# A Fourier block in float32: its products split into three passes, and a residual update moved to GpSimd

## What is computed

```python
def fourier_mix(h, w_o):
    B_, L_, D_ = h.shape
    hg = h.astype(jnp.float32).reshape(B_, L_, FOURIER_GROUPS, FOURIER_GROUP_CH)
    f = jnp.fft.fft2(hg, axes=(1, 3), norm="ortho").real
    return f.reshape(B_, L_, D_).astype(h.dtype) @ w_o
...
def post_norm_update(x, y, mod, j, g, b):
    gate = mod[:, 3 * j + 2][:, None, :]
    return layer_norm(ALPHA * x + gate * y, g, b)
```

## Time and profile before

| what | value |
|---|---|
| median of 3 executions | 2187.61 us (2186.68 to 2189.37) |
| the profiled execution | 2184.68 us |
| its span | 2182.7 us |
| mean granted clock of PE in it | 0.993 |
| PE busy | 2103.3 us, 15744 matmul records |
| DVE busy | 1617.4 us |
| ACT busy | 972.5 us |
| POOL busy | 2.3 us, 8 instructions |

### The profile page before, as it was taken

One profiled execution on the slowest core, in us unless ns is written; L12 is line 12 of the kernel. 1 busy time (PEld: TensorE's weight loads), 2 busy tenths in 40 slices (PEclk: granted clock), 3 DMA queues, 4 the chain that ended last, 5 costly groups with the idle time before them and its releaser, 6 DMA issues. The chain is left out here.

```text
span 2182.7 us, 37144 instructions
## 1 busy us (share of the span) xinstructions
PE 2103.3 (96%) x15744; PEld 1874.4 (86%) x15744; DVE 1617.4 (74%) x2326; ACT 972.5 (45%) x1345; POOL 2.3 (0%) x8
## 2 busy tenths in 40 slices
PE   7999999999999999999999799989999999999998
PEld 5899999887899999977999689889799986768886
DVE  3887877777787788775887778676787776667556
ACT  3434534427543454344434466344454454215443
POOL 0000000000000000000000000000000000000000
PEclk9999999999999999999999999999999999999999
DMA  9866688430689768733988211300388822305541
GB/s 394 331 240 248 235 313 337 155 116 1 248 350 360 298 274 323 309 134 145 366 327 307 67 59 59 136 23 3 126 333 349 339 98 78 116 31 210 209 177 39
DMA packets 65812, 450.83 MB, mean 207 GB/s; under 512 B 7959, under 2 KB 9240, under 8 KB 12696
## 3 DMA queue, kind: packets, MB, share of 16 engines
q1 hardware_dynamic: 65688, 449.11, 53.4%
HBM read 448.03 MB, written 1.05 MB: 206 GB/s over the span
## 5 line engine op out<-in xcount | busy, mean ns | idle before, releaser
L541 PEld LDWEIGHTS banks<-ffn_h_split,ffn_weights_split 128*128 128x128 f32 x6336 | 769.6, 192 | 13.4 <-DVE ffn_weights_split L632 4.7
L541 PE MATMUL banks<-ffn_h_split,ffn_weights_split 128*128 128x256 f32 x6336 | 773.6, 284 | 7.3 <-DVE ffn_h_split L653 6.0
L826 DVE TENSOR_TENSOR ffn_weights_split<-weight_ring,ffn_weights_split 128x2048 fp32r<-128x2048 f32 x223 | 510.4, 2289 | 222.2 <-ACT ffn_weights_split L715 222.2
L715 ACT CAST ffn_weights_split<-weight_ring 128x2048 fp32r<-128x2048 f32 x223 | 424.0, 1901 | 162.7 <-PE banks L559 153.1
L559 PE MATMUL banks<-ffn_weights_split,ffn_hidden_split 128*128 128x512 f32 x1512 | 356.8, 392 | 2.4 <-DVE ffn_hidden_split L752 2.4
L559 PEld LDWEIGHTS banks<-ffn_weights_split,ffn_hidden_split 128*128 128x128 f32 x1512 | 280.9, 189 | 59.2 <-DVE ffn_hidden_split L752 2.8
L782 DVE CUSTOM_DVE_ANT_0 weight_ring<-weight_ring,first_arena,cols 128x1024 f32<-128x1024 f32 x196 | 240.5, 1280 | 0.4 <-ACT first_arena L725 0.4
L679 ACT ACTIVATE ffn_arena<-banks 128x256 f32<-128x256 f32 x132 | 50.6, 383 | 417.3 <-PE banks L541 417.3
L514 PE MATMUL banks<-ffn_h_split,ffn_weights_split 128*128 128x512 f32 x352 | 124.7, 399 | 0.2 <-DVE ffn_h_split L653 0.2
L516 PE MATMUL banks<-ffn_h_split,ffn_weights_split 128*128 128x256 f32 x352 | 98.7, 280 | 0.0
L121 ACT CAST weight_ring_split<-weight_ring 128x2048 fp32r<-128x2048 f32 x34 | 64.5, 1905 | 56.1 <-DMA weight_ring<-in_weights 38.4
(11 more groups left out here) (414 smaller groups left out, 2632.2 us busy)
## 6 DMA issues: line engine op xcount, KB each, us to landing
weight_ring<-in_weights SPq DMA_DIRECT2D x407, 1024.0 KB, 5.0
first_arena<-in_norm_rows SPq DMA_DIRECT2D x12, 512.0 KB, 7.2
first_arena<-in_c_rows SPq DMA_DIRECT2D x4, 512.0 KB, 11.9
first_arena<-in_ctx_rows SPq DMA_DIRECT2D x2, 1024.0 KB
h<-in_ctx SPq DMA_DIRECT2D x1, 1024.0 KB, 17.2
side<-in_x SPq DMA_DIRECT2D x1, 1024.0 KB
x<-in_x_rows SPq DMA_DIRECT2D x1, 1024.0 KB
hyena_tables<-in_hy_filt SPq DMA_DIRECT2D x1, 1024.0 KB
```

The lines of the kernel that those rows point to most:

```text
L541: last = nc.tensor.matmul(bank[:, half * T:half * T + T], w[:, x, sl], hs[:, k, y, :], start=(k == 0 and x + y == 0), stop=(k == DT - 1 an ...
L715: nc.scalar.copy(wsplit[:, c % S, 0, :], raw).then_inc(self.split_hi.sem, 1)
L826: nc.vector.tensor_tensor(wsplit[:, c % S, 1, :], core.wbuf[:, (self.first + at(c)) % NSLOT, :], wsplit[:, c % S, 0, :].bitcast(F32), ALU. ...
```

## The change

In the Fourier block every product but those of the first feature group is made in three passes from split operands. Three new tensors hold high and low parts: `fourier_table_split` (the table), `fourier_h_split` (groups 1 to 3 of `h`) and `fourier_uv_split` (`uv`). ACT makes each high part by a cast (that of `uv` in place of the copy), DVE each low part by a subtraction. `features_whole` is the first group, in plain float32. PE waits for low parts only, by their number in a fixed order (`FOURIER_LOW`). DVE's body no longer refreshes `x`: POOL has a body of its own that does, with the same two instructions (`refresh.on`). ACT's and DVE's other work of the block stands later in their orders.

```diff
     def dve(self, dve, r):
-
-        nc, row = self.core.nc, self.rows[:, r, :].unsqueeze(1).broadcast_to([P, TT, D])
+        self.on(dve, self.core.nc.vector, r)
+
+    def on(self, eng, engine, r):
+
+        row = self.rows[:, r, :].unsqueeze(1).broadcast_to([P, TT, D])
...
-        nc.vector.tensor_tensor(self.x[:, :, :], self.x[:, :, :], row, ALU.mult if r == 0 else ALU.add)\
+        engine.tensor_tensor(self.x[:, :, :], self.x[:, :, :], row, ALU.mult if r == 0 else ALU.add)\
             .then_inc(self.steps.sem, 1)
...
+FOURIER_LOW = {n: i + 1 for i, n in enumerate(("table", "h1", "uv00", "uv01", "h2", "h3", "uv10", "uv11", "uv20", "uv21", "uv30", "uv31"))}
...
+    PASSES = ((0, 0), (0, 1), (1, 0))
...
+        @block.gpsimd
+        def _(pool):
+            refresh.on(pool, nc.gpsimd, 0), refresh.on(pool, nc.gpsimd, 1)
+
         @block.tensor
         def _(pe):
+            def lows(name):
+                pe.wait_ge(low.sem, low.base + FOURIER_LOW[name])
+
+            def features_whole():
+                for t in range(TT):
+                    for k in range(2):
+                        last = nc.tensor.matmul(core.ps[t][:, :], h[:, k, t * P:t * P + P], both(cs[:, k, 0:2, :]),
+                                                start=(k == 0), stop=(k == 1))
+                    last.then_inc(uv_ready.sem, 1)
+
             def features(g):
+                if g == 1:
+                    lows("table")
+                lows(f"h{g}")
                 for t in range(TT):
                     if g >= 2:
-                        pe.wait_ge(uv_copied.sem, uv_copied.base + 2 * (g - 2) + t + 1)
+                        lows(f"uv{g - 2}{t}")
                     for k in range(2):
-                        last = nc.tensor.matmul(core.ps[2 * (g % 2) + t][:, :], h[:, 2 * g + k, t * P:t * P + P],
-                                                cs[:, k, 0:2, :].rearrange("p a n -> p (a n)"),
-                                                start=(k == 0), stop=(k == 1))
+                        for n, (x, y) in enumerate(PASSES):
+                            last = nc.tensor.matmul(core.ps[2 * (g % 2) + t][:, :], hs[:, 2 * g + k, x, t * P:t * P + P],
+                                                    both(css[:, y, k, 0:2, :]), start=(k + n == 0), stop=(k == 1 and n == 2))
                     last.then_inc(uv_ready.sem, 1)
...
         @block.scalar
         def _(act):
-            early.act_weight(act, 0)
+            def h_high(g):
+                nc.scalar.copy(hs[:, 2 * g:2 * g + 2, 0, :], h[:, 2 * g:2 * g + 2, :]).then_inc(high.sem, 1)
+
+            act.wait_ge(tables.sem, tables.base + 32)
+            nc.scalar.copy(css[:, 0, :, :, :], cs).then_inc(high.sem, 1)
+            h_high(1)
             for n in range(2 * G):
                 g, t = n // 2, n % 2
                 if n == 2:
+                    h_high(2), h_high(3)
+                    early.act_weight(act, 0)
+                if n == 4:
                     early.act_weight(act, 1)
...
         @block.vector
         def _(dve):
-            refresh.dve(dve, 0), refresh.dve(dve, 1)
-            early.dve_weight(dve, 0)
...
+            dve.wait_ge(high.sem, high.base + 1)
+            nc.vector.tensor_tensor(css[:, 1, :, :, :], cs, css[:, 0, :, :, :].bitcast(F32), ALU.subtract).then_inc(low.sem, 1)
+            h_low(1)
+            uv_low(0)
+            h_low(2), h_low(3)
+            uv_low(1)
+            early.dve_weight(dve, 0)
+            evacuate(0)
+            uv_low(2)
+            early.dve_weight(dve, 1)
+            evacuate(1)
+            uv_low(3)
+            context.dve_variance(dve)
+            evacuate(2), evacuate(3)
             context.dve_reciprocal(dve)
```

More of the change, by code:

```diff
@@ L1489, in attention, with fourier @@
     core.stage_done()
-def fourier(core, h, out, cs, uv, refresh, context, early, tables):
+FOURIER_LOW = {n: i + 1 for i, n in enumerate(("table", "h1", "uv00", "uv01", "h2", "h3", "uv10", "uv11", "uv20", "uv21", "uv30", "uv31"))}
+def fourier(core, h, out, cs, split, refresh, context, early, tables):
     nc = core.nc
@@ L1499, in fourier @@
     f_ready, f_copied = core.counter("fourier_out_ready"), core.counter("fourier_out_copied")
+    high, low = core.take("operand_high", 4), core.take("operand_low", len(FOURIER_LOW))
+    css, hs, uv = split["table"], split["h"], split["uv"]
     G = D // 256
     pair = lambda g: core.ps[4 + g % 2][:, :].rearrange("p (m t) -> p m t", m=2)
+    both = lambda x: x.rearrange("p a n -> p (a n)")
+    PASSES = ((0, 0), (0, 1), (1, 0))
     with core.block() as block:
@@ L1526, in tokens @@
                         for t in range(TT):
[L1527 to L1530, removed]
+                            for x, y in PASSES:
+                                last = nc.tensor.matmul(core.ps[4 + g % 2][:, m * T:m * T + T],
+                                                        uv[:, g % 2, t, x, part * T + m * P:part * T + m * P + P],
+                                                        css[:, y, t, 2 * part, :], start=(n == 0), stop=(n == 11))
+                                n += 1
                 last.then_inc(f_ready.sem, 1)
             pe.wait_ge(tables.sem, tables.base + 32)
-            features(0)
+            features_whole()
             for g in range(G):
@@ L1559, in _, with h_low, uv_low, evacuate @@
         def _(dve):
-            refresh.dve(dve, 0), refresh.dve(dve, 1)
-            early.dve_weight(dve, 0)
[L1562 to L1567, removed]
+            def h_low(g):
+                dve.wait_ge(high.sem, high.base + g + 1)
+                at = slice(2 * g, 2 * g + 2)
+                nc.vector.tensor_tensor(hs[:, at, 1, :], h[:, at, :], hs[:, at, 0, :].bitcast(F32), ALU.subtract)\
+                    .then_inc(low.sem, 1)
+            def uv_low(g):
+                for t in range(TT):
+                    dve.wait_ge(uv_copied.sem, uv_copied.base + 2 * g + t + 1)
+                    nc.vector.tensor_tensor(uv[:, g % 2, t, 1, :], core.ps[2 * (g % 2) + t][:, :],
+                                            uv[:, g % 2, t, 0, :].bitcast(F32), ALU.subtract).then_inc(low.sem, 1)
+            def evacuate(g):
                 dve.wait_ge(f_ready.sem, f_ready.base + g + 1)
@@ L3253, in first_block @@
                 run(core, project, ffn_a, ffn_b)
-            with phase("fourier", 2048, False):
-                uv = carve(2, TT, 2, T)
+            with nc.sbuf_tensor("fourier_table_split", [P, 2, 2, 3, T], F32R) as table_split, \
+                    nc.sbuf_tensor("fourier_h_split", [P, DT, 2, T], F32R) as fourier_hs, \
+                    nc.sbuf_tensor("fourier_uv_split", [P, 2, TT, 2, 2 * T], F32R) as uv_split:
+                split = dict(table=table_split, h=fourier_hs, uv=uv_split)
                 context = ContextNorm(core, xn, o, vec(2, 1, 1), vec(2, 0, 1), (scale_1, norm("norm1", 2)[0]), tail_small)
                 early = Early(core, side_lo[:, :, :].rearrange("p (k y) t -> p k y t", y=2), 2, False, [(0, 0), (1, 0)])
-                fourier(core, hf, hf, cs, uv, Refresh(core, x, rows), context, early, tables)
+                fourier(core, hf, hf, cs, split, Refresh(core, x, rows), context, early, tables)
                 core.stage_done()
```

15 lines of the change are left out of this document (6 added, 9 removed).

## The result

The changed kernel took 2194.1 us in the median of 16 executions (2190.63 to 2198.75), the kernel before 2188.63 beside it (16 executions, 2185.23 to 2190.54). The ratio is 1.0027, with a 95% interval of 1.002 to 1.0033: slower by some 5.5 us (4.4 to 7.2 by the interval), where 4.2 less were forecast. 2194.1 lies outside the range of 2181.8 to 2190.0 us. Its profiled execution took 2192.56 us at a mean granted clock of 0.988.

What follows compares the result with a forecast made beforehand. The prediction took PE's chain of matmul groups to bound the Fourier block. 4.4 us less PE work minus 0.2 of semaphore delays, the residual costing nothing, gave 4.2 us less: 2187.6 to 2183.4 us, range 2181.8 to 2190.0.

Steps and rivals of the forecast that it cites:

- PE's work: Fourier block's products: split feature groups take 2.74 us, token groups 2.88, together 4.4 us less PE time.
- What has to be ready: Fourier block: ACT's highs and DVE's lows come before PE wants them; costed at 0.2 us of semaphore delays.
- The residual: Refresh of x on POOL: two passes of 4.2 us end well before the block does; costed at nothing.
- rival 2: POOL first at the block's start holds the table's and h 1's lows: 3.3 us slower, 2190.9 us; chance 0.12.
- A rule against the change: Skill's rule that DVE instructions with two SBUF inputs and SBUF-reading GpSimd ones block each other; would give rival 1 or 2.
- the two rivals with turns: Rival 1 and rival 2, in both of which POOL and DVE take turns by whole instructions in the Fourier block.
- Rival 1: POOL, delayed by its ISA instruction, holds DVE's lows in mid-block: gain all but gone, 2187.3 us; chance 0.25.
- Rival 3: No slow start of PE's clock at the Fourier block's border: a gain of 5.6 us, 2182.0 us; chance 0.10.
- Rival 4: POOL ends last, over 20 us ahead of its first addition; 10 us beyond give 2193.4 us; chance 0.05.

Runs made afterwards that it cites:

- e4: The changed kernel with x refreshed on DVE in two free places, the second ring weight's low moved later, POOL without work; 2185.23 us, ratio 0.9982 to the kernel before.
- e3: The changed kernel, with POOL's refresh waiting until DVE has made its last low with two SBUF inputs; 2185.02 us, ratio 0.9984 to the kernel before.
- e6: e4 plus four POOL memsets of 128x2048 from the block's start into a scratch tensor that nobody reads; 2184.88 us in the profiled execution.
- e7: e6 with POOL's four memsets replaced by four copies of the table (128x1536, one SBUF input) into scratch; 2188.52 us in the profiled execution.
- e8: The changed kernel, with DVE making the lows of uv 0 (one PSUM operand) ahead of the table's and h 1's; 2194.38 us in the profiled execution.
- e2: The kernel before with only the refresh of x moved to POOL, products still plain float32; 2188.81 us, ratio 1.0 to the kernel before.
- e5: The changed kernel with POOL's refresh in four additions of 128x1024 instead of two of 128x2048; 2186.78 us, ratio 1.0001 to the kernel before.
- e1: The changed kernel with x refreshed first on DVE, as before, and nothing on POOL in the block; 2187.65 us, ratio 0.9992 to the kernel before.

## Why the prediction was wrong

**PE's work: right.** Features 2.75 us a group (988.59 to 991.34) where 2.74 stood, tokens 2.87 (991.34 to 994.21) where 2.88 stood, and 4.37 us less for the block without POOL (e4).

**What has to be ready: right without POOL.** In e3, at full clock, PE waited 0.31 us where 0.6 stood for a clock of 1.00 from the start, and DVE's lows were 1.76 and 0.68 us. The part called 1.2 us to spare "thin", but only against the clock.

**The residual: this step failed.** It said "Costed at nothing", and looked at one thing alone, whether POOL would be done before the block's end. It was, by 28 us. What it left out is what POOL does to DVE meanwhile: h 1's low ended 11.1 us behind the block's start, where PE wanted it after 3.67, and that cost 7.3 us of idle time and 2.4 us of slow clock (e3 against the change). The rivals had this hold. One of the two reasons given against rival 2 was the ISA instruction ahead of POOL's first addition that "may hold POOL back". Its two records took 11 ns each, and POOL began 0.06 us behind PE. The duration taken for a pass, 4.2 us, was near: 4.53.

**A rule against the change: weighed too lightly.** The other reason was that no row shows any blocking: the trace of before has none in which POOL reads while DVE reads two SBUF operands. But a row that doesn't exist speaks for neither side, and rival 2 was given 0.12. If the engines take turns and POOL is not late, the prediction's own pass of 4.2 us puts the end of h 1 low at 979.7 us, past the 976.4 that decides. So nearly all hung on whether the engines take turns, and the larger chance of the two rivals with turns (0.25) went to a delay of POOL for which no row stood either. The range then ended at 2190.0 us, below the rival's own 2190.9. The Trainium skill ("SBUF — State Buffer", section "Who interferes with whom") says that such a DVE instruction contends with a GpSimd instruction that reads SBUF, and not with one that only writes. The runs agree on each part: memsets beside lows of 1.76 us (e6), copies beside lows of 2.98 (e7), a low with one operand in PSUM at 0.69 (e8).

**Rival 2, term by term.** It had h 1 low end 979.7 - 968.8 = 10.9 us behind the block's start; it ended after 11.1. It had 5.7 us of idle; there were 7.6, because this block had no slow start at its border, so PE arrived at 3.67 and not at 5.2 us. It added a slow start of 1.76 behind the idle; the stretch there cost 2.4. From the full-clock block of e2: 33.28 - 4.4 + 7.6 + 2.4 = 38.9, measured 39.08, so 5.8 us more. The rival's sum of 3.3 was against a block with a slow start; against the profiled one the block grew by 4.13. The medians are 5.5 apart and the ratio gives 5.9; how many executions of before have the slow start isn't known, so the medians can't check the sum more closely than that.

**Rivals 1, 3 and 4.** Rival 1 had the same turns, only later in the block; POOL wasn't late. The hold that it describes did occur in e5, where the lows of h 2 and h 3 took 4.5 us together, and PE didn't wait for them. Rival 3's missing slow start did occur in the profiled execution, but was eaten by the idle time. Rival 4: POOL ended at 979.85, 28.5 us ahead of the last early products' end.

Two versions beat both kernels: e3 (0.9984) and e4 (0.9982). They can't be told from each other. Their gain, 3.5 to 3.9 us by these ratios, is what the forecast promised for a change that has POOL at the block's head.

What stays open: what decides whether PE's clock is low after the idle of 1.9 us at the block's border (it was in the profiled executions of before, e4, e5 and e7, not in those of after, e1, e2, e3, e6 and e8); and how the executions that weren't traced divide between the two starts, which would decide why e1, whose block is 1.8 us longer than e2's at the same start, shows no loss in its median (the intervals of the two ratios overlap).

## What to carry to other kernels

Before work that reads SBUF is moved to GpSimd, list the DVE instructions that run in the same stretch and read two SBUF tensors, and find the one that PE wants first. Each can be held by a whole GpSimd instruction, in turns; the cost is the hold less the time to spare, and it is nothing where that is large (e2) and was several us in the change, where the forecast had 1.2 to spare and a full clock left none. Place the GpSimd work behind the urgent ones with one wait (e3), or keep it on DVE at a place with time to spare (e4); and where PE would idle as long as in e1 (3.4 us) or in the change (7.6), add the slow clock behind the idle, some 2.4 us in this block.

## What the runs showed of the hardware that I had not expected

- A small size is no protection. In e3 two 128x1 instructions on DVE (L1163, all operands in SBUF) took 3.42 us together during POOL's second pass; in e4, with POOL idle, they took 0.35:

```profile
992.61 0.35 DVE L1163 SCALAR_TENSOR_TENSOR small<-small 128x1 f32<-128x1 f32 x2
```

- The turns alternated wherever both engines had an instruction waiting: in the change DVE's low went between POOL's two passes and POOL's second pass went between two lows. In e8, where no low with two SBUF operands had been issued when the first pass ended, POOL's two passes ran back to back, 9.11 us, and the change's took 10.51.
- Idle times of 3.36 (e1), 7.59 (the change) and 7.86 us (e8) on PE were each followed by a features group at the lower clock level, 5.26, 5.18 and 4.96 us instead of 2.75; behind idle times of 0.31 (e3, e6), 1.10 (e7) and 1.56 us (e5) the granted clock was 1.00.
